# Gate scatters moved ahead of the row gathers, four turn buffers, and row copies spread anew in a hybrid attention, state-space and expert-retrieval layer

## The reference, cut to what matters

```python
h = layer_norm(x)                                  # x: (512 tokens, 2048)
z = h @ w_in                                       # q, k, v, ssm_in and two gates
merged = sigmoid(g_attn) * (attention(q, k, v) @ w_attn_up) + sigmoid(g_ssm) * (y_ssm @ w_ssm_up)
h = layer_norm(alpha * h + merged @ w_mix_out)
# PEER: 128*128 single-neuron experts, 8 heads, top 16 of each: 128 picks per token
sc   = (h @ w_q) against sub_keys;  experts, gates = top-k of the sums, softmax
u    = u_table[experts]                            # 128 rows of 2048 per token
act  = gelu(einsum('btd,btrkd->btrk', h, u))
y    = einsum('btrk,btrkd->btd', gates * act, v_table[experts])
ple  = rms_norm(p @ ple_w_in) * sigmoid(h @ w_gate)
out  = layer_norm(alpha * h + y + ple)
```

## Time and profile before

| what | value |
|---|---|
| median of 3 runs | 3922.95 us |
| profiled execution, its own time | 3923.75 us |
| its span from first to last instruction | 3922.0 us |
| mean granted TensorE clock (share of 2.4 GHz) | 0.98 |
| PE busy | 3716.7 us (95%) |
| DVE busy | 2861.8 us (73%) |
| POOL busy | 2252.2 us (57%) |
| output stage on PE, first and last start of L1383 | 1118.8 and 1319.7 us |
| u-stage on PE, first and last start of L1346 | 1718.1 and 2940.0 us |

### The profile page before, as it was taken

The page is one execution under the profiler, slowest core; times in us unless marked ns, Lnnn a source line. Parts: engine busy times, 40 slices in busy tenths (PEclk is TensorE's granted clock), DMA queues, the critical chain, the costliest instruction groups (busy, mean ns, idle before and its releaser), DMA issues.

```text
span 3922.0 us, 49442 instructions
## 1 busy us (share of the span) xinstructions
PE 3716.7 (95%) x17969; PEld 3230.0 (82%) x17969; DVE 2861.8 (73%) x3910; ACT 1142.9 (29%) x1380; POOL 2252.2 (57%) x1262
## 2 busy tenths in 40 slices
PE   6999999999989999999999988888899999999998
PEld 5777887887877788899999888888897888888886
DVE  7666666676752455987778577777657999999998
ACT  3223223224211332232333322222223333333332
POOL 6333333434434244535655788888827888887870
PEclk9999999999999999999999999899999999999999
DMA  6889888887988286999999998888979999999994
GB/s 228 279 279 298 277 285 289 288 291 277 336 302 293 101 305 235 378 337 317 327 320 318 350 358 327 303 321 308 328 286 361 371 379 385 383 386 371 385 373 187
DMA packets 408750, 1228.03 MB, mean 313 GB/s; under 512 B 77464, under 2 KB 122536, under 8 KB 327112
## 3 DMA queue, kind: packets, MB, share of 16 engines
q1 hardware_dynamic: 260920, 766.92, 55.4%
q0 software_dynamic: 63488, 302.31, 20.4%
q10 hardware_dynamic: 84240, 157.63, 11.2%
HBM read 1017.50 MB, written 344.45 MB: 347 GB/s over the span
## 4 chain that ended last, share of the span: by engine, by line
PE 31%; issue 26%; POOL 21%; DVE 9%; DMA 7%; DVEq 4%; SPq 2%; ACT 1%; POOLq 0%; ACTq 0%
POOL wlo L794 8%; POOL gates_d L862 7%; PE bank L1643 5%; PE bank L1644 5%; PE bank L1645 5%; POOL u_row L871 5%; DMA u_rows_d<-u_tout 4%; PE bank L1346 2%; PE bank L1347 2%; PE bank L1348 2%; PE bank L1383 2%; PE bank L1384 2%; PE bank L1385 2%; DVE wlo L1672 2%; DVE u_tout L2227 2%
## 5 line engine op out<-in xcount | busy, mean ns | idle before, releaser
L1346 PE MATMUL bank<-h_hi,whi 128*128 128x384 f32 (+1 forms) x3312 | 1205.2, 364 | 108.6 <-DVE wlo L1672 107.0
L794 POOL TENSOR_TENSOR wlo<-raw,whi 128x1024 fp32r<-128x1024 f32 x268 | 682.6, 2568 | 987.5 <-ACT whi L1001 498.0
L1347 PE MATMUL bank<-h_lo,whi 128*128 128x384 f32 (+1 forms) x3312 | 1191.3, 360 | 0.0
L1348 PE MATMUL bank<-h_hi,wlo 128*128 128x384 f32 (+1 forms) x3312 | 1190.5, 359 | 0.0
L1346 PEld LDWEIGHTS bank<-h_hi,whi 128*128 128x128 f32 x3312 | 633.6, 191 | 174.5 <-DVE wlo L1672 78.9
L1348 PEld LDWEIGHTS bank<-h_hi,wlo 128*128 128x128 f32 x3312 | 632.9, 191 | 50.2
L1347 PEld LDWEIGHTS bank<-h_lo,whi 128*128 128x128 f32 x3312 | 633.4, 191 | 47.8 <-issue 0.2
L1672 DVE TENSOR_TENSOR wlo<-raw,whi 128x2048 fp32r<-128x2048 f32 x254 | 580.0, 2284 | 112.9 <-ACT whi L1310 56.2
L862 POOL DMA_INDIRECT gates_d<-gate_all,place_u x336 | 504.9, 1503 | 188.1 <-issue 179.0
L1643 PE MATMUL bank<-whi,ew_hi 128*128 128x512 f32 x1408 | 549.0, 390 | 6.4 <-DVE wlo L1672 6.2
L1644 PE MATMUL bank<-wlo,ew_hi 128*128 128x512 f32 x1408 | 547.8, 389 | 0.0
(11 more groups left out here) (302 smaller groups left out, 4691.4 us busy)
## 6 DMA issues: line engine op xcount, KB each, us to landing
raw<-in_weights SPq DMA_DIRECT2D x388, 1024.0 KB
v_rows_d<-in_weights ACTq DMA_DIRECT2D x96, 1024.0 KB
tin<-in_weights SPq DMA_DIRECT2D x156, 512.0 KB, 6.5
u_rows_d<-tout SPq DMA_DIRECT2D x312, 256.0 KB, 7.1
u_rows_d<-u_tout SPq DMA_DIRECT2D x200, 256.0 KB
v_rows_d<-in_weights SPq DMA_DIRECT2D x32, 1024.0 KB
gates_d<-zeros SPq DMA_DIRECT2D x32, 768.0 KB, 13.2
act_d<-act_o ACTq DMA_DIRECT2D x128, 192.0 KB
```

The source lines that it names most:

```text
L794: pool.tensor_tensor(wlo[slot][:, part], raw[slot][:, part], whi[slot][:, part].bitcast(F32), ALU.subtract).then_inc(lo_made, 1)
L1346: pe.matmul(bank, whi[slot][:, cols], rhs_hi(c), start=c == 0, stop=False)
L1347: pe.matmul(bank, whi[slot][:, cols], rhs_lo(c), start=False, stop=False)
L1348: last = pe.matmul(bank, wlo[slot][:, cols], rhs_hi(c), start=False, stop=c == DC - 1)
```

## The change

It has five parts, all of them in the order or the place of work; no arithmetic is added or taken away.

1. `u_tout` gets four buffers (the two new ones lie where `h1_hi` and `h1_lo` hold the fourth token tile, unused by then, and where `u_row0` and `u_row1` come later), with four semaphores.
2. The output stage turns 7 slabs, not 9 (1, 3 and 3 ahead of its first three groups on DVE, not 3, 3, 3). SP loads output slabs 2 and 3 without a step behind either. The u-stage turns 52 slabs (4 to 55), so the first dot moves from slab 56 to slab 58.
3. The sums: from slab 11 to 46 three picks in every third slab and one in the others (5 in 3 slabs; before 4 in 3), then three per slab up to slab 56 (before two, later one), then one per slab. All 128 are summed by slab 78, before by slab 106.
4. POOL issues 270 scatters ahead of the first gather, not 200, and then one scatter between two gathers, not three between every two pairs.
5. The row copies of ACT: 12 in the output stage (before none), 42 in the query stage (before 28), 16 in the gate stage (before 24), 18 in the u-stage up to slab 31 (before 36 up to slab 67).

```diff
-UP_STEPS, OUT_STEPS = 16, 9
+UP_STEPS, OUT_STEPS = 16, 7
-TURNED = [len([e for e in TURN_U if e % 2 == k]) for k in range(2)]
+U_TOUTS = 4
+TURNED = [len([e for e in TURN_U if e % U_TOUTS == k]) for k in range(U_TOUTS)]
-GATE_LAYS_AT = HEADS + N_GLU // 2 + N_Q // 2 - 1
-U_LAYS_AT = GATE_LAYS_AT + 6
+OUT_LAYS_AT = 4 * HEADS + 2 * N_GLU
+Q_LAYS_AT = OUT_LAYS_AT + N_OUT - 4
+GATE_LAYS_AT = Q_LAYS_AT + 3 * (N_Q - 2)
+U_LAYS_AT = GATE_LAYS_AT + N_GATE
-FIRST_SCATTERS = 200
+FIRST_SCATTERS = 270
 def scatters_before(k):
-    return min(TD * PICKS, FIRST_SCATTERS + (3 * k + 1) // 2)
+    return min(TD * PICKS, FIRST_SCATTERS + k)
 def sums_by(e):
-    if e < 11:
-        return TOPK
-    return min(PICKS, TOPK + 4 * (e - 10) // 3 if e < 47 else 64 + 2 * (e - 46) if e < 51 else 72 + e - 50)
+    beside_decoding = sum(3 if n % 3 == 2 else 1 for n in range(11, min(e, 46) + 1))
+    return min(PICKS, TOPK + beside_decoding + 3 * max(0, min(e, 56) - 46) + max(0, e - 56))
-    u_tout = [sb(f"u_tout{k}", [P, 4, DC, 32], a_at + (32 + 8 * k) * kb) for k in range(2)]
+    u_tout = [sb(f"u_tout{k}", [P, 4, DC, 32], at) for k, at in
+              enumerate((a_at + 32 * kb, a_at + 40 * kb, w_at + 24 * kb, w_at + 56 * kb))]
...
-            for i in range(3):
+            for i in range(2):
                 load_wide(AT_OUT, i)
                 table_step(HEAD_STEPS + UP_STEPS - 2 + i)
             sp.wait_ge(merged, DC + 1)
             sp.dma_start(b_ln_in[:, :], row(1)).then_inc(ln_in_landed, 16)
-            for i in range(3, N_OUT - 4):
+            for i in range(2, 4):
                 load_wide(AT_OUT, i)
-                table_step(HEAD_STEPS + UP_STEPS - 2 + i)
+            for i in range(4, N_OUT - 4):
+                load_wide(AT_OUT, i)
+                table_step(HEAD_STEPS + UP_STEPS - 4 + i)
...
             for g in range(3):
-                for n in range(3):
-                    x = HEAD_STEPS + UP_STEPS + 3 * g + n
+                for n in range(3 if g else 1):
+                    x = HEAD_STEPS + UP_STEPS + (3 * g - 2 if g else 0) + n
                     turn_slab(x, *turned_in(x))
...
-                n = (e - U_TURN) // 2
+                n = (e - U_TURN) // U_TOUTS
                 dve.wait_ge(raw_landed[e % 2], 16 * ((AT_U + e) // 2 + 1))
                 if n > 0:
-                    dve.wait_ge(tab_stored[e % 2], 64 * n)
+                    dve.wait_ge(tab_stored[e % U_TOUTS], 64 * n)
```

More of the change, by code:

```diff
@@ L440, in build_trunk @@
     tout_stored = [sm("tout_stored0"), sm("tout_stored1")]
-    tab_stored = [sm("tab_stored0"), sm("tab_stored1")]
+    tab_stored = [sm(f"tab_stored{k}") for k in range(U_TOUTS)]
     ya_stored, ya_landed = sm("ya_stored"), sm("ya_landed")
@@ L474, in lay_rows, with lay_nth @@
                             ).then_inc(rows_laid, 16)
+        def lay_nth(queue, n):
+            lay_rows(queue, n // 4, n % 4)
         def tokens(tile, c, n=TT):
@@ L664, in _ @@
                 if e - 2 in TURN_U:
-                    store_rows(u_tout[e % 2], e - 2, tab_stored[e % 2])
+                    store_rows(u_tout[(e - 2) % U_TOUTS], e - 2, tab_stored[(e - 2) % U_TOUTS])
                 if e == 12:
@@ L879, in _ @@
                 pool.wait_ge(tout_stored[k], 64 * TOUTS[k] + 64 * (1 - k))
+            for k in range(U_TOUTS):
                 pool.wait_ge(tab_stored[k], 64 * TURNED[k])
@@ L1189, in _, with queries @@
             up_pair(DC // 2 - 1, True)
-            def queries(start, end, more=None, lays=True):
-                with act.Fori(start, end) as j:
+            def queries(start, end, more=None):
+                for j in range(start, end):
                     for s in range(2):
@@ L1197, in queries @@
                         next_hi(AT_Q, j, s, blk_done, BLK_Q + o)
-                        if lays:
-                            for c in range(2):
-                                lay_rows(act, HEADS + N_GLU // 2 + j, 2 * s + c)
+                        for c in range(3 if o < N_Q - 2 else 0):
+                            lay_nth(act, Q_LAYS_AT + 3 * o + c)
                         act.wait_ge(blk_done, BLK_Q + o + 1)
@@ L1212, in _ @@
                     act.dma_start(res[:, t, :], h0_d[t]).then_inc(res_landed[s], 16)
-            with act.Fori(1, N_OUT // 2) as j:
+            for j in range(1, N_OUT // 2):
                 for s in range(2):
                     next_hi(AT_OUT, j, s, blk_done, BLK_OUT + 2 * j + s)
+                    if j >= 2:
+                        lay_nth(act, OUT_LAYS_AT + 2 * (j - 2) + s)
             def embedding_out(q):
@@ L1256, in _ @@
                 next_hi(AT_GATE, o // 2, o % 2, blk_done, BLK_GATE + o)
-                for n in range(3 * (o // 2) + 2 * (o % 2), 3 * (o // 2) + 2 + o % 2):
-                    lay_rows(act, GATE_LAYS_AT + n // 4, n % 4)
+                lay_nth(act, GATE_LAYS_AT + o)
                 if o % 4 == 0 and o > 0:
@@ L1278, in experts @@
                     if all_four:
[L1279 removed]
+                        lay_nth(act, U_LAYS_AT + s)
                     act.wait_ge(blk_done, BLK_U + e + 1)
@@ L1291, in _ @@
             act.activation(sel_g[:, :, :], sel_g[:, :, :], ACT.Exp).then_inc(exps_made, 1)
-            with act.Fori(0, SB - U_LAYS_AT - 1) as g:
+            experts(1, (SB - 4, 2))
+            with act.Fori(0, 3) as g:
                 for z in range(2):
-                    experts(2 * g + 1 + z, (U_LAYS_AT + 1 + g, 2 * z))
-            with act.Fori(2 * (SB - U_LAYS_AT - 1) + 1, SB) as j:
+                    experts(2 * g + 2 + z, (SB - 3 + g, 2 * z))
+            with act.Fori(8, SB) as j:
                 experts(j)
@@ L2221, in turn_unit @@
             def turn_unit(e):
-                n = (e - U_TURN) // 2
+                n = (e - U_TURN) // U_TOUTS
                 dve.wait_ge(raw_landed[e % 2], 16 * ((AT_U + e) // 2 + 1))
                 if n > 0:
-                    dve.wait_ge(tab_stored[e % 2], 64 * n)
-                dve.transpose(out=u_tout[e % 2][:, :, :, :].rearrange("p e c i -> p c e i"),
+                    dve.wait_ge(tab_stored[e % U_TOUTS], 64 * n)
+                dve.transpose(out=u_tout[e % U_TOUTS][:, :, :, :].rearrange("p e c i -> p c e i"),
                               in_=raw[e % 2][:, :].rearrange("p (c e j) -> p c e j", c=DC, e=4))
```

4 lines of the change are left out of this document (1 added, 3 removed).

## The result

The changed kernel takes 3858.45 us (median of 4, 3846.62 to 3861.97), the kernel before 3922.81 in the same job (median of 4). The ratio is 0.9831, with a 95% interval of 0.9807 to 0.9855. The profiled execution took 3861.94 us, 62 us less than that of before, where 16 were forecast.

What follows compares the result with a forecast made beforehand. POOL's full DMA queue was taken as the path through the u-stage, only reordered by the change: 3923.75 - 14 (output stage) + 92 (later first gather) - 94 (shorter gathers) = 3908 us, range 3862 to 3945.

Steps and rivals of the forecast that it cites:

- +92: u-stage: the first gather comes 92 us later, at 2292 instead of 2200, because more scatters go ahead of it.
- -94: u-stage, first to last gather: 575 us instead of 668, so 94 us shorter; bounds 533 and 627.
- Output stage, -14: Output stage: earlier loads of slabs 3 and 4 save 19.8 us, new waits cost 5.5; gain 14, bounds 6 and 22.
- Turned slabs at 8.4 us: u-stage, slabs 32 to 57: four buffers end DVE's 43.0 us of store waits; slab 58's low part comes at 2209.
- Scatters out by then, 214: u-stage: of 270 scatters 105 are out through slab 31, then 109 at 2.0 us each by 2209.
- The stall, 83 us: Slab 59: PE stops while POOL issues the remaining 56 scatters at 1.4 us each, plus 5 us for a new group.
- A pair of gather and scatter at 4.75 us: u-stage, among the gathers: 4.38 us today, raised to 4.75 for denser DVE and later landings; 114 pairs, 9.0 us a slab.
- Room for about five: POOL's DMA queue: the roughly 4 us gap at every fifth scatter is a wait for earlier ones to land.
- 1 (the sums): Scatters ahead of the gathers: sums or DVE cause their gaps, so the first gather comes near 2201; 3817 us, chance 0.07.
- 2: Scatters ahead of the gathers: queue drains faster without copies (1.6, then 1.25 us); 41 us less, 3867, chance 0.20.
- 3: Stretch with gathers: landings bind it, a pair costs over about 5.0 us; 3936, worst 3988, middle 3955; chance 0.20.
- 4: Output stage: gives nothing because its copies take the gain back, and the rest cancels; 3922 us, chance 0.10.

## Why the prediction missed

The mechanism was the one forecast: POOL's queue is the path, a stall stands in slab 59 with POOL issuing scatters through it, and the stretch behind it is shorter. What failed is the size of two terms: the price of a scatter ahead of the first gather, from which the +92 came, and the price of a pair of gather and scatter, from which the -94 came.

- **Output stage, -14.** Measured -15.1. `b_ln_in` and three loads followed each other, and the wait of 10.4 us went. But its worth isn't its size: alone it gave 2 us, not clear of noise, because it hands two turned slabs to the u-stage and the first gather waits for their store. The working had no term for that wait.
- **Row copies at nothing in query and gate stage.** Right: the gate stage took 174.1 us against 174.3, and the first scatter came 15.3 us earlier, all of it the output stage's.
- **Turned slabs at 8.4 us.** Measured 8.31; slab 58 at 2186, in the time of before 2202 where I had 2209. Most of these 7 us lie ahead of slab 32, which came 12 us earlier in that time and not 6.
- **Scatters out by then, 214.** Measured 220, at 1.84 us in slabs 32 to 57 where I took 2.0. The first step that failed: I stayed near 2.14 since "each store and load stays in the way". Most of the difference is the copies', 2.14 us against 1.84 with them and without. It is worth six scatters, some 8 us.
- **The stall, 83 us.** The mechanism was there as described, 65.3 us: 50 scatters in place of 56 and 1.3 us each, the lower bound's price of 1.25, in place of 1.4 and 5 us for a group of picks. First gather +67 in place of +92. That is 25 of the 46 us that were missed: 7 from slab 58, 8 from the six scatters, 10 from the price in the stall.
- **A pair of gather and scatter at 4.75 us.** First to last gather 553 us and not 575, so (553 - 34) / 114 = 4.56 for a pair. The part is -114.5 and not -94, and this is the other 21 us: the second step that failed. I let POOL's instructions grow by 0.25 us for a pair and added 0.12 for landings. Measured, the two instructions grew by 0.17 (1.83 + 1.98 against 1.95 + 1.69) and the gaps by 0.03 (0.47 + 0.30 against 0.43 + 0.31). So the landings that I charged hardly showed, and the instructions grew by less than DVE's density had made me expect. The new sums may have a part in that; it is not shown. That POOL, and not the transfers, paces the stretch is shown by the kernels without the late scatters and with one-input dots.
- **"Room for about five" as the cause of the pace.** The gap at every fifth DMA is the queue's room, as I had read it. But more room does not make the scatters faster: a queue of seven changed the pattern and not the pace.
- **The rivals.** 1 (the sums) is excluded. 2 was right in the stall (1.3 us, it said 1.25) and not ahead of it (1.84 us, nearer my 2.0 than its 1.6); that its 3867 lies closest to the measured time is partly luck, since the other term was off by 21 us in the same direction. 3 didn't come: the pair stayed under 5.0 us. 4 holds for the output stage alone (3920.8), but not with four buffers beside it (3901.2).

What each part is worth in the changed kernel depends on the others: the order 17 us, the copies' new places 15, the buffers nothing beside 270 scatters and 15 beside 200, the sums about 16 beside 200, this last one not clear of noise. They do not add up to the 64.

Open: why the pace of scatters ahead of slab 32 stays at 2.2 us with the copies gone, what the table loads of ACT do to it, and how much of the 15 us of the enlarged queue is more than the spread of the stretch with gathers, whose length lay between 537 and 553 us in kernels that hardly differ there (two buffers 537.3, copies back 543.4, no wait for sums 550.7).

## What to carry to other kernels

Before pricing a stall or its removal, list every wait in front of the instruction that it releases: the next one may take all that is won, and two edits that each hide the other's wait don't add up. Where a queue is full, ask what an instruction in it would cost alone (0.96 us here against 1.9) and what stands beside it when it is long; moving work to where it is short gave 17 us; making it short everywhere, and not moving it, gave 94 on top. A second input in PSUM is one way, if banks are free.

## What the runs showed of the hardware

- POOL's DMA queue: the gap stands at every fifth DMA with 1024 bytes set aside, mostly at every third with 512, at every seventh with 1408. In the stall, with little else on the DMA engines, there was no gap, with 512 bytes either; there a scatter landed after 2.1 us, beside the other transfers after 7.2 us.
- A dot with its second input in PSUM takes as long as from SBUF (2.28 us), and a DMA of POOL that begins in it takes 0.97 us, where the earlier trace rows had 2.90. One that begins in a low part still takes 2.40 us on average.
- The DMA engines moved 398 GB/s at a share of 1.00 beside a PE at the full clock, where the changed kernel's 377 GB/s at 0.98 had looked like their limit. With the copies late they moved 417 GB/s from 2330 to 2600. A share near 1.00 is no sign that they can carry no more.
- In the stall the granted clock averaged 0.60 over 76 us, in which PE worked 13. When PE worked again it had 0.50 (the level of 1.2 GHz) from 2262 to 2270 and 0.98 from 2270 to 2280.
